# Moving two weight buffers by 64 bytes in a fused three-layer transformer kernel

## The reference, cut to what matters

```python
for i in range(DEPTH):                       # 2 layers
    mod = (c_act @ ada_w[i] + ada_b[i])[:, None, :]
    sh_a, sc_a, g_a, sh_f, sc_f, g_f = jnp.split(mod, 6, axis=-1)
    h = rms_norm(x, norm_g[i, 0]) * (1.0 + sc_a) + sh_a
    y = moba_attention(...) if i % N_MIXERS == 0 else diff_attention(...)
    x = x + g_a * rms_norm(y, norm_g[i, 1])
    h = rms_norm(x, norm_g[i, 2]) * (1.0 + sc_f) + sh_f
    x = x + g_f * rms_norm(swiglu(h, ffn_w_in[i], ffn_w_out[i]), norm_g[i, 3])
# third layer: conformer convolution (pointwise, 31 taps, layer norm, pointwise), then conv_ffn
```

## Time and profile before

| | us |
|---|---|
| median of 3 runs | 984.24 (983.56 to 985.72) |
| the profiled execution | 984.03 |
| its span, first to last instruction | 982.2 |
| PE busy in it | 947.5 (96%) |
| DVE busy in it | 820.6 (84%) |
| ACT busy in it | 544.3 (55%) |

### The profile page before, as it was taken

One profiled execution on the slowest core, in us unless ns is written; L12 is line 12 of the kernel. 1 busy time (PEld: TensorE's weight loads), 2 busy tenths in 40 slices (PEclk: granted clock), 3 DMA queues, 4 the chain that ended last, 5 costly groups with the idle time before them and its releaser, 6 DMA issues. The chain is left out here.

```text
span 982.2 us, 19019 instructions
## 1 busy us (share of the span) xinstructions
PE 947.5 (96%) x6806; PEld 868.6 (88%) x6806; DVE 820.6 (84%) x1217; ACT 544.3 (55%) x1023; POOL 78.0 (8%) x111
## 2 busy tenths in 40 slices
PE   4899999999999999998999999999999999999997
PEld 3899988999999888996999999989997899999996
DVE  4869988898888778777888888889998979988885
ACT  3465546454444566555554444459998555555552
POOL 2100002000000011111300000002240000000000
PEclk9899999999999999999999999999999999999999
DMA  9999983999999965652599999986340549766641
GB/s 347 328 329 349 336 278 97 349 350 343 303 333 322 279 193 162 183 174 84 166 348 359 321 322 317 318 267 173 87 129 1 181 134 301 220 196 192 190 127 43
DMA packets 240770, 234.08 MB, mean 238 GB/s; under 512 B 7497, under 2 KB 208970, under 8 KB 240714
## 3 DMA queue, kind: packets, MB, share of 16 engines
q1 hardware_dynamic: 237824, 226.52, 73.7%
q0 software_dynamic: 1616, 5.32, 1.7%
q10 hardware_dynamic: 1274, 1.52, 0.5%
HBM read 232.27 MB, written 1.06 MB: 238 GB/s over the span
## 5 line engine op out<-in xcount | busy, mean ns | idle before, releaser
L537 PE MATMUL work<-h_hi,whi_a 128*128 128x256 f32 x1360 | 379.0, 279 | 2.8 <-DVE h_lo L1412 2.8
L537 PE MATMUL work<-h_lo,whi_a 128*128 128x256 f32 x1360 | 377.4, 277 | 0.0
L537 PE MATMUL work<-h_hi,wlo_a 128*128 128x256 f32 x1360 | 377.3, 277 | 0.0
L1351 DVE TENSOR_TENSOR wlo_a<-raw,whi_a 128x1024 fp32r<-128x1024 f32 x180 | 218.6, 1223 | 52.2 <-ACT whi_a L1009 51.8
L537 PEld LDWEIGHTS work<-h_hi,whi_a 128*128 128x128 f32 x1360 | 256.3, 188 | 6.4 <-issue 2.9
L537 PEld LDWEIGHTS work<-h_lo,whi_a 128*128 128x128 f32 x1360 | 256.8, 189 | 2.7
L537 PEld LDWEIGHTS work<-h_hi,wlo_a 128*128 128x128 f32 x1360 | 256.4, 189 | 0.0
L1009 ACT ACTIVATE whi_a<-raw 128x1024 fp32r<-128x1024 f32 x180 | 187.9, 1054 | 61.1 <-PE work L537 38.3
L1361 DVE SCALAR_TENSOR_TENSOR acc<-ada_raw,csil,acc 128x1024 f32 (+1 forms) x128 | 163.5, 1279 | 7.2 <-DMA ada_raw<-in_ada_w 5.6
L1009 ACT ACTIVATE whi_b<-raw 128x1024 fp32r<-128x1024 f32 x106 | 110.7, 1055 | 81.4 <-DMA raw<-in_ffn_w_out 42.8
L1351 DVE TENSOR_TENSOR wlo_b<-raw,whi_b 128x1024 fp32r<-128x1024 f32 x106 | 128.5, 1219 | 8.8 <-ACT whi_b L1009 8.6
(11 more groups left out here) (228 smaller groups left out, 1395.6 us busy)
## 6 DMA issues: line engine op xcount, KB each, us to landing
ada_raw<-in_ada_w SPq DMA_DIRECT2D x88, 512.0 KB, 6.4
raw<-in_ffn_w_in SPq DMA_DIRECT2D x88, 512.0 KB, 7.9
ada_raw<-in_mod_w SPq DMA_DIRECT2D x48, 512.0 KB, 6.8
raw<-in_ffn_w_out SPq DMA_DIRECT2D x44, 512.0 KB, 6.2
raw<-in_f_up_w SPq DMA_DIRECT2D x44, 512.0 KB, 4.3
raw<-in_moba_w_qkv SPq DMA_DIRECT2D x24, 512.0 KB, 8.4
raw<-in_diff_w_qkv SPq DMA_DIRECT2D x24, 512.0 KB, 8.0
raw<-in_a_pw_w SPq DMA_DIRECT2D x24, 512.0 KB, 7.4
```

The lines of the kernel that those rows point to most:

```text
L537: mm = pe.matmul(dst, w[u][:, ws], h[:, k, :], start=(k == 0 and m == 0), stop=(k == KT - 1 and m == 2))
L1351: dve.tensor_tensor(wlo[u], raw[:, u, :], whi[u].bitcast(F32), ALU.subtract).then_inc(lo[u], 1)
```

## The change

The small tensors `relt` and `ssy` (32 and 16 bytes a partition) move up behind `colB`, so that 192 bytes, not 128, stand ahead of `whi_b`; a spacer of 192 bytes goes in ahead of `h_hi`. No instruction is added, removed or moved.

```diff
         csil = sb("csil", [P, 16])
         colA = sb("colA", [P, KT])
         colB = sb("colB", [P, KT])
+        relt = sb("relt", [32, H])
+        ssy = sb("ssy", [P, 2 * TT])
         whi_b = sb("whi_b", [P, 4, D], F32R)
         wlo_b = sb("wlo_b", [P, 4, D], F32R)
         ada_raw = sb("ada_raw", [P, 4, D])
         acc = sb("acc", [P, 6 * D])
         xt_eps = sb("xt", [P, TT, D + 1])
         xs_pad = sb("xs", [P, TT, D + 1])
+        sb("spacer14", [P, 48])
         h_hi = sb("h_hi", [P, KT, S], F32R)
...
         mix = sb("mix", [P, 2692])
         cols = sb("cols", [P, COLS])
-        relt = sb("relt", [32, H])
-        ssy = sb("ssy", [P, 2 * TT])
         taps0 = sb("taps0", [P, 72])
```

More of the change, by code:

```diff
@@ L95, in build @@
         ab_hi0 = sb("ab_hi0", [P, PADW], F32R)
-        sb("spacer18", [P, 32])
+        sb("spacer21", [P, 32])
         ab_hi1 = sb("ab_hi1", [P, PADW], F32R)
-        sb("spacer20", [P, 32])
+        sb("spacer23", [P, 32])
         ab_lo0 = sb("ab_lo0", [P, PADW], F32R)
-        sb("spacer22", [P, 32])
+        sb("spacer25", [P, 32])
         ab_lo1 = sb("ab_lo1", [P, PADW], F32R)
```

## The result

The changed kernel takes 995.77 us (median of 4 runs, 995.11 to 996.65) against 984.23 before; the ratio is 1.0116, 95% interval 1.0098 to 1.0133. It is slower by 11.5 us, above the range that was forecast (977.2 to 990.0), and on the side of two of the rivals.

A forecast was written before the change was run, and what follows sets the result against it. The prediction took PE, the number of matmuls by their pace, to bound the kernel. All terms were 0 except attention's -1.0 us: 984.03 - 1.0 = 983.0 us, range 977.2 to 990.0.

The forecast's parts named there:

- two of the rivals: The two slower ones: row products get dearer (990.0 us, chance 0.26) and loop projections turn slow (996 us, chance 0.06).
- the projections' term: Projection matmuls: operand distance 192 before and after, so cost nothing unless they are entered in another way.
- the loop's projections turn slow: Feed-forward loops: row products leave PE in the slow phase, 66 steps x 0.20 us = +13 us, 996 us; chance 0.06.
- the step from values to projections changes it: Attention: claimed the pace changes where projections follow values; seven of eight such projections run slow.
- The second step: Row products (1080 matmuls, bounds -5.8 to +7.0 us) and values (384, bounds -0.4 to +1.2): distance becomes 0, both taken as 0.
- the faster rival: Row products lose their 5.4 ns excess per matmul: 977.2 us, or 980 for half; chance 0.29 wholly or half.
- the bound of +1.2 us: Values in attention: the cost if all their blocks turn slow, 288 x 4.2 ns.
- the dearest row pace: Row products: about 6.5 ns over the usual per matmul, 1080 x 6.5 = +7.0 us, giving 990.0 us.
- The gain in attention, -1.0 us: Seven slow projections behind values go fast, 7 x 0.20 us = -1.4 us, taken as -1.0; bounds -1.4 and 0.
- The jolt from values to projections: Attention: the moving operand's step from 128 to 192, which the change makes 192 to 192; thought to slow seven projections.

The follow-up runs named there:

- the break: The changed kernel plus one small one-column float32 matmul between row product and first projection in the feed-forward loops: 997.08 us, ratio 1.0123.

## Why the prediction was wrong, point by point

**The bound was read rightly.** Time is the number of matmuls by their pace, and the four terms of the table above give back 11.4 of 11.9 us. DVE, ACT and the loads played no part.

**The step that failed is the projections' term, put at nothing** because their own distance stays 192. It measured +13.2 us, more than the whole change of 11.5. A matmul's distance doesn't fix its pace: at 192 a projection has 113.3 or 117.8 ns, and the block ahead decides which. The prediction had left a door open ("unless they are entered in another way") and priced it as a rival, *the loop's projections turn slow*, with a chance of 0.06. I had seen in the trace that a block can hand a slow pace on, and then argued it away: the moving operand wouldn't jump on leaving a row product. The jump has nothing to do with it. With the jump and with the last load of the kernel before, the run with the rows at 128 is slow all the same, and in the run with the weights at 192 and the rows at 0 there is no jump, and both paces occur. That the rival's +13 us is so near the measured +13.2 is partly luck: it counted 66 steps, the loops have 60 and cost 12.1 us, and the rest came from attention and around it, which the rival left out.

The evidence was also thinner than the prediction says. Its slow projections weren't only those behind values: in the kernel before one is slow behind small float32 matmuls (from 58.56), and of the two blocks of values that were slow, one was followed by a fast projection and the other (from 353.13) by a slow one. So "the step from values to projections changes it" was no rule.

**The second step is the value 0 for the row products and the values**, and the reason given for it, "because the row with distance 0 is at the normal pace". That was a single load beneath a projection. A pace is something a block settles into over several matmuls, and one of them doesn't show it: in the changed kernel's loop the first five row matmuls of a product take 233, 236, 228, 233 and 231 ns, and only then come 226 and 227. Settled, distance 0 gives 512 columns 226.7 ns (the whole excess of 5.4 ns gone, as the faster rival had it) and 256 columns 119.8 ns. Because of the first five, the row products gained 3.9 us and not 5.8. For the values the bound of +1.2 us was also too small, since it was taken from the slow pace of 117.9; they cost +1.9.

**The rivals were added up as if they excluded each other.** Two of them came together, cheaper rows and slow projections, and that was no accident: with all rows at distance 0 the second followed from the first in each of the five kernels tried, and in the sixth, with its last matmul cut in two; only the break between them parted the two. The range stopped at 990.0, the dearest row pace, because the slow loop, at 996, was left out as unlikely.

**The gain in attention, -1.0 us, had the wrong sign.** The jolt from values to projections did go, but the values now run at 119.8 ns, and leave the projection slow as before (5.65 us in the timeline).

**The rule of the Trainium skill.** "SBUF — State Buffer", section "Who interferes with whom", says that PE's moving operand and its weight load have independent ports and that PE never waits on anyone. The runs don't agree with what the prediction drew from it, that no distance between the two operands could matter: a shift of the two weight buffers by 64 bytes cost 1.0%, and one of `h_hi` and `h_lo` by 64 bytes 2.3%. By that reading the result would have been 984.0.

**What stays open.** Shown: the paces depend on distances (the shift of everything changes none), a phase is handed on (both paces at the same addresses, and the break, behind which the loop's projections are fast). Not shown: what in PE or SBUF makes the phases, why a settled 227 ns leaves the slow one, and why rows at distance 64, which don't settle there, leave it too, and what decides the phase behind a wait or behind small matmuls. That the two reads of PE meet modulo 256 is a reading of these results; no run tried another modulus.

## What to carry to other kernels

When PE is the bound and its operands are fp32r, place can matter: in this one kernel moves of 64 to 192 bytes cost up to 2.3% and gained at most 0.2%. So read the pace (start to start) of each kind of matmul after every change of the SBUF layout, that of kinds that weren't touched first. Don't judge a distance by one matmul: take a block of twelve or more. And price together the pace of a block and what it does to the next: here the cheapest row product came with the dearer loop, and rows laid out with mixed distances were best, by 0.16%. A layout can also leave the phase open, and then the executions of one kernel scatter (986 to 993 us in one run here).

## What the runs showed of the hardware that was not expected

- fp32r matmuls of 256 columns have two settled paces at distance 192 here, 113.3 and 117.8 ns, and 119.8 ns at distance 0. The values had 117.7 at distance 64 (weights and rows both at 0), and 118.7 and 119.6 at 128 (the input at 0, weights and rows both at 64), as means over the span. Of 512 columns: 226.7 at distance 0, 233.3 at 192 (steady, or 231 and 236 in turn) and 233.3 at 128 (229 and 238 in turn).
- With the weights at 192 and the rows at 0, the pace of 48 matmuls went with the last row matmul ahead of them: slow behind 230 or 231 ns, fast behind 233 to 236. It is no rule for other layouts: in the loop of the kernel before they are fast behind 228 or 229.
- One small float32 matmul between row product and projection, some 0.1 us, made all 60 projections of the changed kernel's loops fast. Elsewhere projections behind small float32 matmuls came in either phase.
